# Routing stage: a token tile's product split around the turns and router products of the tile before it

## The reference, cut to what matters

```python
h = h + gt1[:, None, :] * mix               # mix = y @ w_out; the second block has no gate
m_in = modulate(rmsnorm(h, norm2_g[l]), sh2, sc2)
grp_logits = (hf @ w_router_grp)            # 4 groups
exp_logits = (hf @ w_router_exp)            # 32 (16) experts
...                                         # best group, its two best experts, their weights
for e in experts:
    out += combine[:, e] * (silu(hf @ wg[e]) * (hf @ wu[e])) @ wd[e]
```

## Time and profile before

| | us |
|---|---|
| median of 3 runs | 1429.84 (1424.71 to 1432.71) |
| the profiled execution's own time | 1430.29 |
| its span in the trace | 1428.5 |
| routing stage of the first `moe`, from its first products to the first expert products | 363.3 to 446.7 |
| routing stage of the second `moe`, from its first product to the first expert products | 1059.9 to 1152.0 |

### The profile page before, as it was taken

The page is one execution under the profiler, slowest core; times in us unless marked ns, Lnnn a source line. Parts: engine busy times, 40 slices in busy tenths (PEclk is TensorE's granted clock), DMA queues, the critical chain, the costliest instruction groups (busy, mean ns, idle before and its releaser), DMA issues. The chain is left out here.

```text
span 1428.5 us, 19238 instructions
## 1 busy us (share of the span) xinstructions
PE 1334.8 (93%) x7784; PEld 631.0 (44%) x7784; DVE 574.8 (40%) x1230; ACT 332.3 (23%) x574; POOL 120.1 (8%) x278
## 2 busy tenths in 40 slices
PE   4999998999898996698999999999999999999997
PEld 2555546864454332233474444444444543333332
DVE  7849545545554331121758971001124532111106
ACT  5422432432111110010455641110001111110113
POOL 4100000001001110110200024000000000101000
PEclk9999999999998997899999999999999979999999
DMA  9711111074826899999741112211046368999995
GB/s 373 331 60 60 60 59 60 3 269 174 324 80 271 362 423 423 423 423 380 283 177 59 59 59 81 95 59 74 0 148 264 148 250 312 421 389 424 387 420 191
DMA packets 41226, 316.39 MB, mean 221 GB/s; under 512 B 7102, under 2 KB 7110, under 8 KB 21168
## 3 DMA queue, kind: packets, MB, share of 16 engines
q1 hardware_dynamic: 32808, 296.34, 51.9%
q0 software_dynamic: 7872, 17.73, 3.3%
q10 hardware_dynamic: 456, 1.08, 0.2%
HBM read 303.16 MB, written 22.56 MB: 228 GB/s over the span
## 5 line engine op out<-in xcount | busy, mean ns | idle before, releaser
L2770 PE MATMUL mix_ps<-y_t,store 128*128 128x512 f32 (+1 forms) x640 | 249.7, 550 | 1.4 <-ACT y_t L2851 1.4
L2770 PEld LDWEIGHTS mix_ps<-y_t,store 128*128 128x128 f32 x640 | 121.4, 190 | 127.2 <-issue 124.0
L2170 PE MATMUL m_ps<-store,par 128*32 128x512 f32 (+2 forms) x896 | 151.0, 597 | 0.0
L2170 PE MATMUL mix_ps<-store,par 128*32 128x512 f32 (+2 forms) x688 | 120.4, 618 | 27.2 <-DMA store<-in_gu 15.4
L1121 PE MATMUL mix_ps<-y_t,store 128*128 128x512 f32 x320 | 142.7, 599 | 0.0
L1121 PEld LDWEIGHTS mix_ps<-y_t,store 128*128 128x128 f32 x320 | 59.2, 190 | 71.6 <-issue 70.7
L2170 PEld LDWEIGHTS m_ps<-store,par 128*32 128x32 f32 (+2 forms) x896 | 47.0, 120 | 83.4 <-issue 83.4
L2300 DVE TENSOR_TENSOR m2r_a<-m2r_a,m_ps 128x256 f32<-128x256 f32 x22 | 9.3, 421 | 178.2 <-ACT m2r_a L2224 178.2
L3088 DVE TENSOR_TENSOR store<-store,m_ps 128x512 f32<-128x512 f32 x8 | 5.5, 687 | 183.5 <-PE m_ps L3072 183.5
L2170 PEld LDWEIGHTS mix_ps<-store,par 128*32 128x32 f32 (+2 forms) x688 | 37.0, 123 | 94.6 <-issue 94.6
L2192 PE MATMUL m_ps<-store,m2r_a 128*32 128x512 f32 (+2 forms) x448 | 76.3, 595 | 1.4 <-issue 0.9
(11 more groups left out here) (729 smaller groups left out, 1860.6 us busy)
## 6 DMA issues: line engine op xcount, KB each, us to landing
store<-in_gu SPq DMA_DIRECT2D x54, 2048.0 KB, 15.8
store<-in_dn SPq DMA_DIRECT2D x54, 1024.0 KB, 16.7
store<-in_w_in SPq DMA_DIRECT2D x14, 2048.0 KB, 11.0
store<-in_w_ada SPq DMA_DIRECT2D x12, 2048.0 KB, 9.8
mods<-in_gu SPq DMA_DIRECT2D x10, 2048.0 KB
mods<-in_dn SPq DMA_DIRECT2D x10, 1024.0 KB
store<-in_w_out SPq DMA_DIRECT2D x4, 2048.0 KB, 8.3
store<-y_rows SPq DMA_DIRECT2D x8, 1024.0 KB, 9.6
```

Source lines behind the costliest of these rows:

```text
L2170: last = pe.matmul(ps[who, 2 + j % 2, :], xt[:, k, who], w[:, k, :], start=(k == 0), stop=(k == KD - 1))
L2770: last = pe.matmul(pz[:, n % 4, cols], w[:, k, j * P:(j + 1) * P], m.a_t[:, k, cols], start=(k == 0), stop=(k == KD - 1))
```

## The change

`logits(t)` is cut into `turn_x(t)` (the turns), `logits(t)` (the router products) and `turn_logits(t)` (the logits' turn). `product(n)` takes a range of steps. For tiles 0, 1 and 2 the product n = 2t + 3 is put around the three: two of its steps behind the turns, one behind the router products, five behind the logits' turn. Counts and ranks of tiles 0 and 1 now stand ahead of the next tile's turns instead of behind its logits' turn. Tile 3 keeps its order. On VectorE `add_product(2t + 2)` moves ahead of `top_two(t)`, and `add_product(2t + 3)` stays behind it.

```diff
-        def product(n):
+        def product(n, k0=0, k1=KD):
             t, q = n // 2, n % 2
-            if t == 0:
+            if t == 0 and k0 == 0:
                 m.stream.wait(pe, chunk0 + q)
-            if n >= begun + 2:
+            if n >= begun + 2 and k0 == 0:
                 pe.wait_ge(ev, n - 1)
...
-            for k in range(KD):
+            for k in range(k0, k1):
...
+            if k1 < KD:
+                return
...
-            if t == NT - 1:
-                keep_clock(1, HALF)
+
+        def logits(t):
+
...
+        def turn_logits(t):
+
             pe.wait_ge(lg_out, t + 1)
             pe.transpose(ps[:, 5, t * NL:(t + 1) * NL], flat_t[:], m.ident[0:NL, 0:NL]).then_inc(logit, 1)
+
+        def logits_within(t, n):
+
+            turn_x(t)
+            product(n, 0, 2)
+            logits(t)
+            product(n, 2, 3)
+            turn_logits(t)
+            product(n, 3)
...
-        logits(0)
-        product(3)
+        logits_within(0, 3)
         product(4)
-        logits(1)
         counts(0)
         ranks(0)
-        product(5)
+        logits_within(1, 5)
         product(6)
-        logits(2)
         counts(1)
         ranks(1)
-        product(7)
+        logits_within(2, 7)
         counts(2)
         ranks(2)
+        turn_x(3)
+        keep_clock(1, HALF)
         logits(3)
+        turn_logits(3)
...
+        add_product(0)
+        add_product(1)
         for t in range(NT):
-            add_product(2 * t)
-            add_product(2 * t + 1)
...
             if t < NT - 1:
                 turned(t)
+                add_product(2 * t + 2)
             top_two(t)
+            if t < NT - 1:
+                add_product(2 * t + 3)
```

More of the change, by code:

```diff
@@ L1764, in product, with turn_x @@
                 last.then_inc(mm, 1)
-        def logits(t):
-            s = slice(t * P, (t + 1) * P)
+        def turn_x(t):
             for h in range(2):
@@ L1785, in logits @@
                     pe.wait_ge((ev_a, ev_v)[k // 4], t + 1)
-                last = pe.matmul(ps[0:NL, 4, 0:P], w_lg[:, k, :], m.y_t[:, k, s], start=(k == 0), stop=(k == KD - 1))
+                last = pe.matmul(ps[0:NL, 4, 0:P], w_lg[:, k, :], m.y_t[:, k, t * P:(t + 1) * P], start=(k == 0),
+                                 stop=(k == KD - 1))
             last.then_inc(flat_lg, 1)
+        def turn_logits(t):
             pe.wait_ge(lg_out, t + 1)
             pe.transpose(ps[:, 5, t * NL:(t + 1) * NL], flat_t[:], m.ident[0:NL, 0:NL]).then_inc(logit, 1)
+        def logits_within(t, n):
[5 more added lines that the diff above has]
+            product(n, 3)
         def keep_clock(bank, *widths):
```

## The result

The changed kernel takes 1419.66 us (median of 6 runs, 1413.10 to 1422.41), the kernel before 1428.00 beside it (6 runs). The ratio on record is 0.9933, 95% interval 0.9914 to 0.9953: 0.67% faster, and at least about 0.5%. (The quotient of the two medians alone is 0.9942, a difference of 8.3 us; by the ratio it is 9.6.) The profiled execution took 1421.97 us with a span of 1420.2, 8.3 us shorter than the one before.

What follows compares the result with a forecast made beforehand. TensorE, busy 1334.8 of 1428.5 us, was taken as the bound. Savings of 5.1 us (first stage's tile 0) and 3.7 (five tiles), 8.8 together, took 1430.29 to 1421.5, 1421.0 for the median; range 1417 to 1427.

Steps and rivals of the forecast that it cites:

- The overlap: Split tiles: product steps hide the 0.34 and 0.36 us gaps; about 0.45 us of wait stays at first stage's tile 0.
- rival 4: Split tiles: another wait (`both_r`, `ev`) replaces the hidden one at each tile; 1428 to 1430 us, chance 0.07.
- The ordinary tile: Five tiles, all split ones but first stage's tile 0: 3.80 us becomes 3.06, saving 0.74 each, 3.7 in all.
- (b): Ordinary tile: two product records, then the switch to router products, 0.96 us; the switch adds 0.09.
- (d): Ordinary tile: switches from router products to a product and from a product to the logits' turn, 0.15 us together.
- Counts and ranks: Tiles 0 and 1: moved ahead of the next turns, they cost the same 0.4 us and wait for nothing.
- Tile 0 of the first stage: First routing stage: shorter wait and full clock save 5.1 us, 2.0 if the clock still falls.
- The earlier addition on VectorE: `add_product(2t + 2)` ahead of `top_two`: waits for nothing, lies in VectorE's idle time, and product 2t + 4 needs it.
- What passes on: Behind product 7 both stages stay as before; the DMA-bound expert stretch starts earlier, so all 8.8 us pass on.
- Rival 2: First expert stage: DMA-bound stretch fixed in time hides the first stage's gain, leaving 2.2 us; 1427.6 us, chance 0.07.
- Rival 3: Split tiles: TensorE drains at each of 24 new switches, 0.46 us each, 11.0 in all; 1430.6 us, chance 0.04.
- Rival 1: Half clock in or behind routing stages shifts: 1424 to 1426 us, chance 0.22; lucky side 1416.5 to 1418.5, chance 0.10.

Runs made afterwards that it cites:

- one cut fewer: Changed kernel with three product steps behind the turns and none between router products and logits' turn, then five steps; one run, 1418.68 us.
- the extra filler: Changed kernel plus tile 0's copies ahead of the norm and Sqrt, with more unread matmuls at both stages' ends; 1418.77 us, ratio 0.9934 to the kernel before.

## Why the prediction was right

The forecast was 1421.0 us, measured were 1419.66; the range held. The forecast started from the three runs of before (1429.84); beside the changed kernel before took 1428.00, so against the 8.8 us forecast stand 8.3 by the medians and 9.6 by the ratio. Point by point:

- *The overlap.* Right. Of the waits of TensorE in the split tiles only the one at tile 0 is left, 0.39 us where I said 0.45. No other wait took its place (rival 4), and nothing waits for counts and ranks.
- *The ordinary tile*: the term was too large, 0.74 us against 0.46 to 0.56, 2.6 us in five tiles instead of 3.7. Its pieces in the rows of the second stage: turns 0.91 as said; the product's 32 records, in three runs of 4, 2 and 26, take 1.81 + 1.06 + 11.35 = 14.22 from start to start, against 13.82 in two unbroken products, so the cuts cost 0.40 where (b) and (d) gave 0.24; the router records 1.86 where I had 1.75. Together 0.27. The experiment with one cut fewer puts the middle cut at 0.12.
- *Counts and ranks* in a place of their own: I said nothing; the kernels that keep the old block but have them there take up to 0.16 us more for a tile. Inside the 0.5 us of an ordinary tile this is already paid.
- *Tile 0 of the first stage.* 4.92 us against 5.1 in this pair of traces. But the step "the clock in the products 2.19, in the second half 0.9" is not a constant of the kernel before: with the same orders on TensorE and the same wait, the clock fell in two traces (22.70 and 22.78) and stayed full in two (19.63 and 19.74). In both traces with the fall it came 4.2 us behind the first turn, as the wait ended. Certain are 1.9 us, and up to 3.1 more come where the fall would have been. The sum booked these 3.1 as if every execution had them, because the one trace of before did; what share of executions has them, four traces can't say. The forecast had luck here.
- *The earlier addition on VectorE.* Right, and needed: with the old place the tiles lose 1.4 and 0.5 us each and the ratio is 0.9988. By itself it does nothing. The closeness at tile 2 held: counts(2) follows product 7 without a wait.
- *What passes on.* Right: the stretch from the first expert to the second stage is 633.44 us against 633.85, so the DMA-bound expert stage started and ended earlier together. In 12 of the 14 traces it is 633.4 to 634.4 us, though the first expert starts anywhere from 440.7 to 448.5. The two others are the 636.24 and 631.37 of the sections above. Rival 2 is refuted.
- *Rival 3*, a drained engine at each switch, would have given 0.46 a switch; the cuts show about 0.1, which is also less than a load of 0.19. The rule of the Trainium skill (TensorE: Matmul & The Clock Gate, Part 3) on weight loads was rightly left out of the sum: the run of 26 full-height records takes 11.35 us, 0.437 each, with a load of 190 ns within.
- *Rival 1, on its lucky side*, came true beside the forecast. All five kernels without the extra filler that gain 0.9 to 1.6 us in the second stage's tiles have 21.1 to 23.0 us from product 7 to the first expert; all eight others have 24.2 to 24.4, also the one with the split in the first stage only. What sets them apart is where the clock falls, counted from the start of the work behind product 7. In the eight it falls after 12.2 to 13.1 us and stays at half for some 17, into the first expert. With the split in the second stage only it falls after 11.1 us and is back before the first expert. In the four others it falls after 13.5 to 14.3 us and is back some 3 us later; with one cut fewer it then stays full, and in the other three it falls again after 21 us, just ahead of the first expert, which takes 9.6 to 10.0 us there. That is worth 1.3 to 3.2 us, and in two kernels some 3 us more in the first expert, and made up for the 1.1 us that the ordinary tiles fell short.

So the overlap was forecast rightly, and the closeness of the time is in part luck. The sum had 1.1 us too much in the ordinary tiles and up to 3.1 too much at tile 0 in executions without the fall, and it left out some 2 us of clock at the end of the second stage, which I hadn't put in the likeliest case. One of the prediction's own signs of being wrong, a clock that falls behind the stages otherwise than before, did appear, to the good side. Why the clock falls at one of these places in the second stage and not at another isn't shown. In the eight kernels it stayed at 12.2 to 13.1 us behind product 7 though their t0 lay anywhere from 371.4 to 373.6, and no run shifted the stage without changing its work.

## What to carry to other kernels

Cutting a long accumulation to put small dependent steps between its parts pays when the hidden wait is well over 0.1 to 0.2 us, the price of a cut here (the middle cut costs 0.12 us, and cutting two products into three runs 0.40 in all); take the additions that free its banks along, or the wait comes back. Before a split is used to cover a long wait, look at what stands ahead of the awaited instruction in its own queue, on each engine that delivers a part: two reordered copies alone took tile 0 to 17.89 us, the split to 17.78 (in the traces; in time the copies alone couldn't be told from no change). And where the trace of before shows a fall of the clock, profile again before it is booked as a gain.

## What the runs showed of the hardware

- With the same wait of 1.72 to 1.73 us at the same place, the granted clock fell to half for almost 7 us in two traces and stayed full in two. The Trainium skill (TensorE: Matmul & The Clock Gate, Part 1) says of the start of a kernel that the number of matmuls at the slow clock varies from run to run of one kernel. The traces agree on the start, with 1.03 or 1.85 us for the same eight matmuls; that a fall in the middle of a kernel varies too is what these four traces add.
- A run of two 128x512 records between small matmuls takes 1.06 us from start to start, one of four 1.81, one of 26 11.35: a constant of 0.1 to 0.2 us a run over the records' own pace of 0.429 (a run of 10 takes 4.49, so 16 records more take 6.86).
- Filler work meant to keep the clock up costs up to double once the clock is down: ten 512-column records took 7.06 and 7.58 us in the two stages, against an estimated 4.4 at the pace of 0.429, and the turns behind them started 22.4 and 22.7 us after product 7, against 19.5 and 18.8 without the extra filler.
